# First weights in two transfers, GpSimd's loads behind them; parameters transposed between x's blocks, state space steps one part earlier

## The reference

```python
xn = rmsnorm(x, norm_mix_g)                      # (256, 2048)
proj = xn @ w_in                                 # 2048 x 5120, cut into the heads' inputs
# SB   : stick-breaking attention, 8 heads of 64:
#        w = exp(log_sigmoid(z) + sum of log_sigmoid(-z) behind), strictly causal
# S5   : lam_bar = exp(lam * dt);  b_bar = (lam_bar - 1) / lam * b
#        state_t = lam_bar * state_(t-1) + b_bar u_t    (32 groups x 64 complex states)
#        y = Re(c . state) + d * u;  y = gelu(y);  y = y * sigmoid(y @ w_glu + b_glu)
# DIFF : softmax map 0 - lambda * softmax map 1, 8 heads of 2 x 64
h = x + concat[rmsnorm(SB), rmsnorm(S5), rmsnorm(DIFF) * 0.8] @ w_out
t = rmsnorm(h, norm_ffn_g)
# top-1 of 4 expert groups, then top-2 of its 8 experts
out = rmsnorm(h + sum_e gate_e * (silu(t @ w1_e) * (t @ w3_e)) @ w2_e, final_norm_g)
```

## Time and profile before

| | us |
|---|---|
| median of 3 runs | 1445.14 |
| lowest and highest | 1442.19, 1447.92 |
| the profiled execution | 1447.03 |
| its span, first to last instruction | 1444.9 |
| TensorE busy (PE) | 1370.9 (95%) |
| VectorE (DVE), ScalarE (ACT), GpSimd (POOL) busy | 540.0, 345.2, 224.0 |
| mean granted clock of TensorE | 0.983 |

### The profile page before, as it was taken

How to read it: one execution, slowest core, us unless ns; L and a number is a source line. 1 busy time by engine, 2 the same in 40 slices (tenths; PEclk the granted TensorE clock), 3 DMA queues, 4 the chain that set the end, 5 groups by cost and what they waited for, 6 DMA issues and landing times.

```text
span 1444.9 us, 19175 instructions
## 1 busy us (share of the span) xinstructions
PE 1370.9 (95%) x7248; PEld 774.6 (54%) x7248; DVE 540.0 (37%) x1023; ACT 345.2 (24%) x618; POOL 224.0 (16%) x203
## 2 busy tenths in 40 slices
PE   7999999998999999998999999999999999899896
PEld 6884898986786445334533543434544543443353
DVE  5999421415525323313313323223323332332225
ACT  1121378465563111211111111011111020111002
POOL 2001756785683000000000000000000000000000
PEclk9999999999999999999999999999999999999988
DMA  8433543343375799999999999959999999999991
GB/s 211 174 117 117 204 175 117 121 172 117 120 276 245 310 429 427 428 428 427 428 429 429 428 428 429 428 225 431 429 429 428 429 428 429 428 428 429 428 425 78
DMA packets 71373, 471.66 MB, mean 326 GB/s; under 512 B 17297, under 2 KB 17378, under 8 KB 46114
## 3 DMA queue, kind: packets, MB, share of 16 engines
q1 hardware_dynamic: 70674, 469.75, 79.3%
q10 hardware_dynamic: 528, 1.05, 0.2%
q0 software_dynamic: 128, 0.26, 0.1%
HBM read 468.95 MB, written 2.10 MB: 326 GB/s over the span
## 4 chain that ended last, share of the span: by engine, by line
PE 62%; DMA 18%; DVE 4%; ACT 2%; issue 1%; DVEq 0%; POOL 0%; POOLq 0%; ACTq 0%
PE ps L1831 25%; DMA ring<-in_expert_w_dram 18%; PE ps L1849 11%; PE ps L1494 11%; PE ps L1809 5%; PE ps L1839 3%; PE ps L1860 2%; PE ps L1861 2%; PE ps L1821 1%; DVE reg_e L1125 0%; DVE reg_y L1087 0%; PE ps L1656 0%; ACT reg_s L772 0%; DVE reg_x L1429 0%; PE ps L1614 0%
## 5 line engine op out<-in xcount | busy, mean ns | idle before, releaser
L1849 PE MATMUL ps<-ring,reg_y 128*64 128x512 f32 x1056 | 238.7, 605 | 9.7 <-DVE reg_y L1344 7.8
L538 POOL TENSOR_TENSOR w_lo<-ring,w_hi 128x512 fp32r<-128x512 f32 x152 | 197.5, 1329 | 87.4 <-ACT w_hi L597 85.8
L1350 DVE TENSOR_TENSOR y_lo_t<-ps,y_hi_t 64x512 fp32r<-64x512 f32 x132 | 90.9, 689 | 215.0 <-ACT y_hi_t L829 213.7
L1849 PEld LDWEIGHTS ps<-ring,reg_y 128*64 128x64 f32 x1056 | 75.4, 139 | 146.6 <-issue 142.6
L829 ACT ACTIVATE y_hi_t<-ps 64x512 fp32r<-64x512 f32 x132 | 78.0, 591 | 318.0 <-PE ps L1849 315.5
L1359 DVE TENSOR_TENSOR reg_x<-ps,reg_x 128x512 f32<-128x512 f32 x136 | 87.3, 684 | 137.4 <-PE ps L1861 137.4
L1831 PE MATMUL ps<-reg_e,reg_s 128*64 128x512 f32 x528 | 119.5, 594 | 12.2 <-POOLq L560 11.5
L1831 PE MATMUL ps<-ring,reg_s 128*64 128x512 f32 x528 | 120.0, 596 | 6.9 <-POOLq L560 6.4
L1831 PE MATMUL ps<-ring,reg_y 128*64 128x512 f32 x528 | 120.0, 596 | 6.8 <-POOLq L560 6.2
L1831 PE MATMUL ps<-reg_e,reg_y 128*64 128x512 f32 x528 | 121.5, 602 | 2.9 <-POOLq L560 2.1
L1339 DVE TENSOR_SCALAR reg_y<-ps,lamv 128x512 f32<-128x512 f32 x33 | 24.8, 751 | 241.9 <-PE ps L1831 241.9
(11 more groups left out here) (379 smaller groups left out, 1769.5 us busy)
## 6 DMA issues: line engine op xcount, KB each, us to landing
ring<-in_expert_w_dram SPq DMA_DIRECT2D x128, 2048.0 KB, 20.5
reg_e<-in_expert_w_dram SPq DMA_DIRECT2D x64, 2048.0 KB, 20.6
ring<-in_w_in_dram SPq DMA_DIRECT2D x20, 2048.0 KB, 8.0
ring<-in_w_out_dram SPq DMA_DIRECT2D x8, 2048.0 KB, 7.9
reg_x<-in_x_dram SPq DMA_DIRECT2D x4, 1024.0 KB, 8.5
out_dram<-reg_x SPq DMA_DIRECT2D x4, 512.0 KB, 2.7
reg_e<-in_ssm_w_glu_dram ACTq DMA_DIRECT2D x1, 1024.0 KB, 9.1
reg_e<-in_final_norm_g_dram SPq DMA_DIRECT2D x1, 1024.0 KB, 11.8
```

The lines of the kernel that those rows point to most:

```text
L538: G.tensor_tensor(w_lo[:, i % BUFS, :], unit(u % SLOTS_A)[:, c, :], w_hi[:, i % BUFS, :], ALU.subtract).then_inc(row_lo, 1)
L1350: last = V.tensor_tensor(y_lo_t[64 * q:64 * q + 64, w], psb[3 + k // 2][64 * (k % 2):64 * (k % 2) + 64, :], y_hi_t[64 * q:64 * q + 64, w], ...
L1849: last = M(psb[3 + i // 2][64 * (i % 2):64 * (i % 2) + 64, :], hT[:, 2 * half + f, :], unit2(s)[:, f, 512 * i:512 * i + 512], start=half = ...
```

## The change

The first unit of w_in comes in two transfers of four rows each, with a semaphore for the first; TensorE waits for the two halves apart, and GpSimd waits for the first half before it issues B's loads. At the start TensorE transposes six banks of block 0, three of block 1, then the parameters (into `at[2]`), then does the row sum, then the state space parameters (`at[2]` too), then the rest; bank 6, which is `at[2]`, and bank 7 come last. DVE copies the state space parameters before its 16 evacuations. `S_STEP` (but its first) and `Y_STEP` are one less, and so `P_GLU`, `P_SB`, `P_SBN`, `P_DF` and `P_DFN` are 38, 42, 55, 57 and 71. Otherwise ACT's order is as before.

```diff
--- before.py
+++ after.py
@@ -72,8 +72,8 @@
 R0 = 72
 X_ORDER = [(R0 + i) % DC for i in range(DC)]
 P_BT = 4
-S_STEP = [9] + [15 + 27 * k // 10 for k in range(ST // 2 - 1)]
-Y_STEP = [17 + (27 * k + 9) // 10 for k in range(ST // 2)]
+S_STEP = [9] + [14 + 27 * k // 10 for k in range(ST // 2 - 1)]
+Y_STEP = [16 + (27 * k + 9) // 10 for k in range(ST // 2)]
 P_GLU = Y_STEP[-1] + 3
 P_SB = P_GLU + 4
 P_SBN = P_SB + 3 * (SBH // 2) + 1
@@ -263,6 +263,7 @@
         achain = sem("achain")
         xsum = sem("xsum")
         eps_set = sem("eps_set")
+        w0_in = sem("w0_in")
         rms_diag = sem("rms_diag")
         rms_mm = sem("rms_mm")
         tr_evac_v = sem("tr_evac_v")
@@ -451,7 +452,12 @@
                         sp.wait_ge(row_used, 8 * (n - SLOTS_A + 1))
                     else:
                         sp.wait_ge(row_lo, 8 * (n - SLOTS_A + 1) - R0)
-                sp.dma_start(slot(s).rearrange("p (c n) -> p c n", n=src.shape[-1]), src).then_inc(ring_in[s], 16)
+                dst = slot(s).rearrange("p (c n) -> p c n", n=src.shape[-1])
+                if n == 0:
+                    sp.dma_start(dst[:, 0:4, :], src[:, 0:4, :]).then_inc(w0_in, 16)
+                    sp.dma_start(dst[:, 4:8, :], src[:, 4:8, :]).then_inc(ring_in[s], 16)
+                else:
+                    sp.dma_start(dst, src).then_inc(ring_in[s], 16)
                 if n == 1:
                     later_parameters()
                 if n == 12:
@@ -520,6 +526,7 @@
             G.memset(bnat[:, :, :, :], 0.0).then_inc(b_zero, 1)
 
             g.wait_ge(b_zero, 1)
+            g.wait_ge(w0_in, 16)
             for k, b in enumerate((b_re, b_im)):
                 bv = b.rearrange("l (j h) n c -> (l h) n j c", h=2)
                 for h in range(2):
@@ -580,7 +587,7 @@
             a.wait_ge(rstd_s, 1)
             A.activation(rmsc[:, 4:6], rmsc[:, 2:4], ACT.Sqrt).then_inc(achain, 1)
             a.wait_ge(pT_done, 1)
-            A.activation(pcol[:, 0:49], at[3][:, 0:49], cp).then_inc(pT_evac, 1)
+            A.activation(pcol[:, 0:49], at[2][:, 0:49], cp).then_inc(pT_evac, 1)
             a.wait_ge(rms_mm, 1)
             A.activation(rms_b, at[3][:, T:2 * T], cp).then_inc(rms_row, 1)
             row = [R0]
@@ -903,6 +910,8 @@
             v.wait_ge(lam_in, 16 * 3)
             V.tensor_copy(spar[:, 2, :].rearrange("p (h n) -> p h n", h=2),
                           dt2[:, :].unsqueeze(2).broadcast_to([ST, 2, 64])).then_inc(sp_done, 1)
+            v.wait_ge(sT_done, 1)
+            V.tensor_copy(sw[:, 0:3, :], at[2][:, 64:64 + 3 * ST].rearrange("p (k j) -> p k j", j=ST)).then_inc(sp_read, 1)
             v.wait_ge(pT_evac, 1)
             v.wait_ge(rms_row, 1)
             for c in range(DC):
@@ -911,8 +920,6 @@
                 V.scalar_tensor_tensor(act_x[:, c, :], psb[c // 2][:, (c % 2) * T:(c % 2) * T + T], g_mix[:, c:c + 1], rms_b,
                                        ALU.mult, ALU.mult).then_inc(tr_evac_v, 1)
 
-            v.wait_ge(sT_done, 1)
-            V.tensor_copy(sw[:, 0:3, :], at[1][:, 0:3 * ST].rearrange("p (k j) -> p k j", j=ST)).then_inc(sp_read, 1)
             v.wait_ge(sp_read, 1)
             R = lambda i: sw[:, i, :]
             exp_rows(R(16), R(2), R(5), R(6), R(7), ki[:, :])
@@ -1442,33 +1449,33 @@
                     last = TR(psb[m][:, k2 * T + b * P:k2 * T + b * P + P], xt[:, b, c * P:(c + 1) * P], ident[:, :])
                 return last
 
-            last_m = DC // 2 - 1
             pe.wait_ge(x_in[0], 16)
-            for m in range(last_m):
+            for m in range(6):
                 x_transposes(m, 0)
+            pe.wait_ge(x_in[1], 16)
+            for m in range(3):
+                x_transposes(m, 1).then_inc(tr_done, 1)
             pe.wait_ge(par_in, 16 * 7)
             for i in range(3):
-                TR(at[3][:, 16 * i:16 * i + 16], prow[:, i, :], ident[0:16, 0:16])
-            TR(at[3][:, 48:49], prow[0:1, 3, :], ident[0:1, 0:1]).then_inc(pT_done, 1)
-            pe.wait_ge(x_in[1], 16)
-            for m in range(last_m):
+                TR(at[2][:, 16 * i:16 * i + 16], prow[:, i, :], ident[0:16, 0:16])
+            TR(at[2][:, 48:49], prow[0:1, 3, :], ident[0:1, 0:1]).then_inc(pT_done, 1)
+            pe.wait_ge(cst, 2)
+            pe.wait_ge(rms_diag, 1)
+            M(at[3][:, T:2 * T], ones[:, :], rms_d.rearrange("p b t -> p (b t)"), start=True, stop=True).then_inc(rms_mm, 1)
+            pe.wait_ge(sp_done, 1)
+            pe.wait_ge(pT_evac, 1)
+            for i in range(3):
+                last = TR(at[2][:, 64 + 16 * i:80 + 16 * i], spar[:, i, :], ident[0:16, 0:16])
+            last.then_inc(sT_done, 1)
+            for m in range(3, 6):
                 x_transposes(m, 1).then_inc(tr_done, 1)
-                if m == 2:
-                    pe.wait_ge(cst, 2)
-                    pe.wait_ge(pT_evac, 1)
-                    pe.wait_ge(rms_diag, 1)
-                    M(at[3][:, T:2 * T], ones[:, :], rms_d.rearrange("p b t -> p (b t)"), start=True, stop=True).then_inc(rms_mm, 1)
+            pe.wait_ge(sp_read, 1)
+            x_transposes(6, 0)
+            x_transposes(6, 1).then_inc(tr_done, 1)
             pe.wait_ge(rms_row, 1)
-            x_transposes(last_m, 0)
-            x_transposes(last_m, 1).then_inc(tr_done, 1)
-
-            def s_transpose():
-
-                pe.wait_ge(tr_evac_v, 12)
-                pe.wait_ge(sp_done, 1)
-                for i in range(3):
-                    last = TR(at[1][:, 16 * i:16 * i + 16], spar[:, i, :], ident[0:16, 0:16])
-                last.then_inc(sT_done, 1)
+            x_transposes(7, 0)
+            x_transposes(7, 1).then_inc(tr_done, 1)
+
             def b_transpose(n_):
 
                 if n_ == 0:
@@ -1504,7 +1511,9 @@
             def native_row(n_, cc, banks):
 
                 u = 2 * n_ + cc // 8
-                if cc % 8 == 0:
+                if u == 0 and cc == 0:
+                    pe.wait_ge(w0_in, 16)
+                if cc % 8 == (0 if u else 4):
                     pe.wait_ge(ring_in[u % SLOTS_A], 16 * (u // SLOTS_A + 1))
                 if n_ == 0:
                     pe.wait_ge(tr_evac_v, max(cc + 1, 4))
@@ -1677,7 +1686,6 @@
 
 
             steps = [[] for _i in range(8 * NB)]
-            steps[0].append((s_transpose,))
             for k in range(2):
                 steps[3 + k].append((c_transpose, k))
             for k in range(8):
```

## The result

The changed kernel took 1452.09 us, the median of 6 runs (1448.91 to 1454.06), against 1446.42 (1442.19 to 1447.92) beside it: ratio 1.0037, interval 1.0025 to 1.0049. Repeated with the later experiments it took 1452.98 (1446.71 to 1457.03, 8 runs) against 1446.84: 1.0038, interval 1.0023 to 1.0054. So it is slower by 5.7 us, which lies inside the half per cent I had called no change. I forecast +9.25.

A forecast was written before the change was run, and what follows sets the result against it. TensorE's own sequence was taken to bound the front half, with shifts passing one to one to the end. Start +0.1, GLU +4.7 and norm +4.45 gave +9.25 on 1445.14, so 1454.4 us; range 1442 to 1459.

The forecast's parts named there:

- (b): Rival: the waits at the moved steps come but the clock stays high; +5.45, 1450.6 us; chance 0.15.
- (c): Rival: the start's lead is kept, DVE being ready for the second s_in; +4.5, 1449.7 us; chance 0.07.
- Part 1: The start: first w_in rows begin at about 14.9, 2.7 us earlier; TensorE ahead by about 4.6 us at row 8.
- Part 2: DVE's chain at the start: state space parameters copied ahead of the evacuations put it ahead by 4.2 us.
- Part 3: State space steps one part earlier: TensorE waits 3.3 us for DVE's product at second s_in; +0.1 net of the start.
- Part 4: GLU one part before block 4's end: TensorE waits 3.4 us for row 84's w_lo; +4.7 with the clock.
- Part 5: Stick-breaking norm's sum one part before block 6's end: TensorE waits 2.85 us for ACT's square; +4.45 with the clock.
- The clock: Slow matmuls behind each of three new waits: 1.3 us each in Parts 3 and 4, 1.6 in Part 5.
- (e): Rival: a drain of about 1.38 us after the GLU's table load lengthens ACT's chain; 1455.8 us; chance 0.02.
- (a): Rival: block ends cost nothing, ACT and POOL being far enough ahead; not slower, 1444.8 us; chance 0.16.
- (d): Rival: a further wait for w_in units landing late, about 5 us more, 1459; chance 0.10.

The follow-up runs named there:

- run 6: Kernel before with only w_in's first unit in two transfers, TensorE waiting for each half, B's loads behind the first: 1442.55 us, ratio 0.9971.
- run 7: The change's order of transposes and parameters alone, first unit in one transfer, B's loads at once, steps as before: 1445.53 us, ratio 0.9992.
- run 8: Run 1 without GpSimd's wait, so the unit in two transfers but B's loads issued at once: 1441.25 us, ratio 0.9955.
- run 3: The change with P_GLU and all later places one part later, as before; only s_in and s_y stay early: 1443.68 us, ratio 0.9978.
- run 4: The change with P_SB and all behind it one part later, as before; the GLU stays one part early: 1449.77 us, ratio 1.0023.
- run 10: The change with 21 unused matmuls filling TensorE's waits for row 84's w_lo and ahead of the norm's sum: 1450.20 us, ratio 1.0025.
- run 11: The changed kernel, unaltered, measured and profiled once more on the same chip: 1452.98 us, ratio 1.0038 to the kernel before.
- run 5: The change with ACT's evacuations of blocks 4 and 6 moved behind the squares, all steps still one part early: 1445.70 us, ratio 0.9996.
- run 2: Kernel before with only the steps (S_STEP, Y_STEP and what follows from them) one part earlier, old start: 1455.47 us, ratio 1.0070.
- run 9: Run 1 with the norm's sum one part early, block 6's evacuation behind the square, df_tr in its old place: 1441.06 us, ratio 0.9962.
- run 1: The change with S_STEP, Y_STEP and what follows from them as in the kernel before, so only the start is new: 1440.38 us, ratio 0.9965.

## Why the prediction came out as it did

The order of mechanisms was right: the start brings 5 us, the moved steps cost more than that, and the experts pass the rest on (with 0.8 and 1.6 us more in the two profiles). The range holds the result. My forecast of 1454.4 is 2.3 us above the median and 3.6 above in the difference to before; it had the change slower by more than half a per cent, which did not come. The result lies between that case and rivals (b) and (c), each of which came true in part.

- **Part 1.** First matmul at 14.21, forecast 14.9; it varies by execution, from 14.08 to 15.32 in the nine profiles with this order of loads. I had DVE begin at 12.75; it began at 12.40, since the row sum took 0.67 us, where I had kept the 1.06 of before. The measured gain of the start (5.1 ± 2.4) agrees with 4.6. What I had not separated: the two transfers carry it, and no gain of B's order is shown (runs 6 to 8).
- **Part 2.** 4.67 instead of 4.2; 0.35 of the difference is the same.
- **Part 3, the mis-sized term.** I put the product's end at L1046, 77.45, with 0.57 us to spare. The releaser is L1040, the multiplication, which ended at 73.76 + 2.36 = 76.12 (L1047 now); the sums behind it are not what s_in waits for. With that row, the lead of 5.4 that TensorE had at the first s_in (50.67 against 56.04) and DVE's 4.67, the forecast would have read: TensorE at 69.2, product at 71.45, wait 2.2. Measured: 2.22. At the third s_in, too, I wrote "no slack at all" where L1040 had ended 1.36 us ahead (83.46 + 2.35 = 85.81 against 87.17). So 2.5 us of lead were kept instead of 0 to 0.8, and rival (c), kept lead, came true by half. That DVE sets this point is seen in runs 3, 4 and 10: TensorE began w_in 0.7 to 1.1 us later there, waited 1.11 to 1.18, and the second s_in went at 71.45 to 71.50 all the same. "Busy without a gap" told that DVE was the limit, but not which of its instructions released TensorE. The wait list of before couldn't give it, since there was no wait; the semaphore in the code (`s_prod`) and the row of L1040 could.
- **Part 4.** Wait 3.14, forecast 3.4; with the clock +6.5 ± 2.5, forecast 4.7. The largest cost, as said.
- **Part 5.** Wait 2.64, forecast 2.85; with the clock +2.0 ± 2.5, forecast 4.45. The wait was right; of its cost about 0.2 us came back at df_tr (1.17 against 1.36 in run 4). The interval reaches from nothing to the forecast, so the term's size is open.
- **The clock.** I charged 1.3, 1.3 and 1.6 us as if it fell behind each wait. It does so only in some executions: behind all three in run 11, behind the sum only in the first profile; in run 4 behind w_lo, in run 5 behind the s_in wait, in run 2 behind the sum and not behind w_lo. In run 11 the forecast's working can be tested whole, since the clock fell behind all three. TensorE ends the last projection part ahead of the act_lo wait (a wait of 2.06 us in each of these kernels) at 339.62 - 2.06 = 337.56, before at 330.72 - 2.06 = 328.66:

```profile
339.62 0.47 PE L1501 MATMUL ps<-w_hi,act_hi 128*128 128x512 f32 x1 [2.06 <-DVE act_lo L1164]
```

  That is +8.9; the forecast said +9.25. That it comes so near is luck, since two errors of mine cancel inside it: more lead was kept at the product (Part 3), and the slow stretch behind that wait took 3.4 us and not 1.3, so that the third s_in went at 83.86, with nothing of the lead left (87.17 - 3.46 - 83.86 = -0.15). In the first profile it is 335.65 - 2.06 = 333.59, +4.9. It lost 4.9 us less to the clock up to there (1.4 against 6.3) and is 4.0 ahead of run 11, since it had to wait 0.47 at the third s_in and run 11 did not, among smaller things.
- **What the sum left out.** Behind 330 us the gap shrinks by 3.9 us, to +5.0 in run 11 and +1.1 in the first profile (first gather of the experts at 469.57 and 465.62, before at 464.54). The profiled execution of before lost 1.7 us to the clock behind the act_lo wait, the two of the changed kernel nothing:

```profile
335.65 5.72 PE ps L1501 x24
```

  That answers the 7.29 of the earlier trace rows. From 330 to 480 us before lost 8.1 us to the clock, the changed kernel 6.6 in both, which is 1.5 of the 3.9. Another 2.2 are two waits that the profile of before has and the two of the changed kernel don't: 1.00 at df_tr and 1.19 in the router:

```profile
358.59 0.55 PE L1656 MATMUL ps<-ident,reg_e 128*128 128x128 f32 x3 [1.00 <-DVE reg_e L1140]
```

```profile
460.32 0.19 PE L1785 MATMUL ps<-reg_s,before_b 128*128 128x32 bf16 x1 [1.19 <-DVE reg_s L1244]
```

  Both belong to the execution as much as to the kernel. The router's wait stands in the four profiles where the slow stretch ahead of it cost 1.7 us (before, runs 6, 9 and 10) and is missing in the nine where it cost 3.4: TensorE was then later than DVE. I took the slow stretches and waits of one execution as given and only added new ones. The wait of 2.06 for act_lo shows how much that is worth: it stands in all 13 profiles of this case, and a slow stretch follows it at once in six (before, runs 3, 4, 5, 6 and 8). Whether the changed kernel would lose it again in other executions, two profiles can't say: this part stays open, and 3.9 us of the forecast hang on it.

In the changed kernel the sigmoid follows its table load at once: the load at 181.84 ends at 183.12 and the sigmoid starts at 183.14. The Trainium skill, page "ScalarE: Activation LUTs", section "What ACT_TABLE_LOAD costs", gives 1.28 us for the load, which agrees, and about 1.38 more for a drain, which no row here shows. So rival (e) fell. Rival (a) fell with the two waits, and for (d) no w_in unit behind the first kept TensorE waiting.

The best version is the change with its steps back (run 1, 1440.38), equal within the intervals to runs 8 and 9: by the ratios 5 us below before and 10 below the change.

## What to carry to other kernels

When a gain at the start moves TensorE ahead, the fixed steps behind it don't have to move with it: list for each step which instruction of which engine releases it and how long before, and move only those that have room. The releaser must be read off the semaphore that the waiting instruction names in the code (here that of the multiplication), since a wait list without the wait doesn't show it. Where another engine takes up a step's chain only behind the last row of a block, the matmuls that TensorE has left to do cover that chain. Taking one part of them (2.87 us) away cost about the whole part here, 3.14 us at the GLU and 2.64 at the norm, and changing the order on ACT (square ahead of evacuation) took both waits away.

## What was unexpected of the hardware

- The same wait of TensorE is followed by a slow clock in one execution of a program and not in another: 2.22 us at 71 us (clock 1.00, and 0.50 from 73 to 76), 3.1 us at the GLU (1.00, and 0.55). The wait of 2.06 for act_lo was followed by one in six of 13 profiles. Up to 480 us a slow stretch cost 1.4 to 1.7 us, or 3.0 to 3.4 where it lasted about twice as long. A profiled execution can so stand several us from the median by the clock alone: 3.2 below it in the first profile of the change, and the two profiles of the change are 4.7 apart in span and 4.7 in clock loss.
- The clock fell to half behind idle stretches as short as 1.90 us (run 5, at 71 us) and 2.06, and at the sum it stayed up where TensorE was kept busy through the same time (run 10).
- The four loads of B, 64 KB each, issued into the first 2 MB of weights, made its two halves land later (9.0 us from issue against 7.0 to 7.5), and yet TensorE did not wait for them (run 8). What moved the start was reading the unit in two transfers: first matmul at 15.02 instead of 17.59, although the transposes ahead of it ran at half the clock.
